# Forty instead of thirty-two tokens of an expert layer on fetched rows, and low parts of value units made in pairs

## What is computed

```python
u_g = peer_u[ic]                                   # rows picked by each token
h = gelu(einsum('chkd,cd->chk', u_g, xc)) * gc     # dot, GELU, gate
v_g = peer_v[ic]
out = einsum('chk,chkd->cd', h, v_g)               # sum of value rows
```

## Time and profile before

| | |
|---|---|
| median of 3 runs | 987.57 us |
| the profiled execution | 987.29 us, span 985.5 us |
| busy: TensorE, VectorE, ScalarE, GpSimd | 99%, 75%, 64%, 61% of the span |
| expert units | about 296 to 650 us, the gated ones from 470 |
| value units | about 650 to 978 us |
| granted clock of TensorE | 1.00 up to the last microseconds |

### The profile page before, as it was taken

The page is one execution under the profiler, slowest core; times in us unless marked ns, Lnnn a source line. Parts: engine busy times, 40 slices in busy tenths (PEclk is TensorE's granted clock), DMA queues, the critical chain, the costliest instruction groups (busy, mean ns, idle before and its releaser), DMA issues.

```text
span 985.5 us, 22607 instructions
## 1 busy us (share of the span) xinstructions
PE 975.0 (99%) x7344; PEld 918.3 (93%) x7344; DVE 743.3 (75%) x1718; ACT 626.6 (64%) x1232; POOL 598.1 (61%) x292
## 2 busy tenths in 40 slices
PE   9999999999999999999999999999999999999997
PEld 8998899999899999999999999989999999999996
DVE  7664663544747797887788888879888878888886
ACT  6774375556556666676988888865555555555553
POOL 3685624687318999989777777874443335444420
PEclk9999999999999999999999999999999999999999
DMA  7463303355545555555554444499888887988871
GB/s 264 141 238 121 128 35 107 129 188 195 204 162 171 210 203 208 211 201 209 188 189 170 170 170 170 171 355 383 311 317 316 317 309 280 333 317 313 305 276 44
DMA packets 61821, 215.05 MB, mean 218 GB/s; under 512 B 7203, under 2 KB 9251, under 8 KB 61644
## 3 DMA queue, kind: packets, MB, share of 16 engines
q1 hardware_dynamic: 51980, 180.04, 51.0%
q0 software_dynamic: 9216, 33.56, 9.4%
q10 hardware_dynamic: 576, 0.82, 0.2%
HBM read 212.89 MB, written 1.06 MB: 217 GB/s over the span
## 4 chain that ended last, share of the span: by engine, by line
PE 96%; POOL 2%; DVE 1%; ACT 1%; DMA 0%; issue 0%; ACTq 0%; DVEq 0%; POOLq 0%
PE PS L988 21%; PE PS L922 21%; PE PS L993 12%; PE PS L926 11%; PE PS L493 4%; PE PS L494 4%; PE PS L495 4%; PE PS L871 3%; PE PS L503 2%; PE PS L879 2%; PE PS L948 1%; POOL lo L1509 1%; PE PS L949 1%; PE PS L657 1%; PE PS L507 1%; PE PS L912 1%
## 5 line engine op out<-in xcount | busy, mean ns | idle before, releaser
L1509 POOL TENSOR_TENSOR lo<-raw,hi 128x1024 fp32r<-128x1024 f32 x191 | 459.4, 2413 | 152.7 <-ACT hi L1069 139.2
L922 PE MATMUL PS<-xb,hi 128*128 128x448 f32 x1024 | 235.0, 371 | 0.0
L1069 ACT CAST hi<-raw 128x1024 fp32r<-128x1024 f32 x203 | 212.7, 1048 | 33.2 <-DMA raw<-in_u_units 12.4
L988 PE MATMUL PS<-xb,hi 128*128 128x448 f32 x1008 | 228.7, 368 | 0.0
L922 PEld LDWEIGHTS PS<-xb,hi 128*128 128x128 f32 x1024 | 183.0, 189 | 12.2
L988 PEld LDWEIGHTS PS<-xb,hi 128*128 128x128 f32 x1008 | 179.9, 189 | 11.8
L2176 DVE TENSOR_TENSOR lo<-raw,hi 128x1024 fp32r<-128x1024 f32 x126 | 154.1, 1223 | 24.2 <-ACT hi L1406 24.1
L1443 ACT CAST xb<-arena 128x224 fp32r (+1 forms) x126 | 47.9, 380 | 143.6 <-PE PS L993 142.3
L926 PEld LDWEIGHTS PS<-xb,lo 128*128 128x128 f32 x1024 | 133.8, 191 | 4.7 <-POOL lo L1509 0.7
L993 PEld LDWEIGHTS PS<-xb,lo 128*128 128x128 f32 x1008 | 132.7, 191 | 4.1
L1406 ACT CAST hi<-raw 128x1024 fp32r<-128x1024 f32 x128 | 133.9, 1046 | 3.4 <-DMA raw<-in_v_units 3.4
(11 more groups left out here) (353 smaller groups left out, 1517.0 us busy)
## 6 DMA issues: line engine op xcount, KB each, us to landing
raw<-in_u_units SPq DMA_DIRECT2D x128, 512.0 KB
raw<-in_v_units SPq DMA_DIRECT2D x128, 512.0 KB
raw<-in_w_in_units SPq DMA_DIRECT2D x43, 512.0 KB
raw<-in_w_q_units SPq DMA_DIRECT2D x16, 512.0 KB
raw<-in_w_proj_units SPq DMA_DIRECT2D x8, 512.0 KB
raw<-in_w_out_units SPq DMA_DIRECT2D x8, 512.0 KB
arena<-bias_rows SPq DMA_DIRECT2D x2, 512.0 KB, 5.0
arena<-in_subkeys_t SPq DMA_DIRECT2D x1, 1024.0 KB, 5.4
```

The source lines that it names most:

```text
L922: mm(o[:, 0:2 * TD].rearrange("p (s t) -> p s t", s=2), hi[:, w, P * k:P * k + P], xb[:, k, :, 0:TD], start=(k == 0), stop=False, skip_gro ...
L988: return mm(PS[:, V_BANKS[c], 0:2 * TD].rearrange("p (s t) -> p s t", s=2), hi[:, (U_V + j) % 4, P * c:P * c + P], coef_slot(u + j)[:, :, ...
L1069: nc.scalar.copy(hi[:, j, :], raw[:, j, :]).then_inc(hi_made, 1)
L1509: nc.gpsimd.tensor_tensor(lo[:, w, :], raw[:, w, :], hi[:, w, :].bitcast(F32), ALU.subtract).then_inc(lo_pool, 1)
```

## The change

- Tokens on fetched rows: 40, in groups of 32 and 8. TD becomes 216, wide matmuls 432 columns, low ones 216. The units with gate products are 54 instead of 56 (68 to 121); FIRST stays 68, GATED_UNITS 60.
- Rows and picks of 32 tokens are repeated 4 times as before, those of 8 tokens 16 times. On SyncE's queue, at the same place, stand 3 + 15 copies of rows and 4 + 16 of picks, 38 transfers instead of 7.
- 80 fetches, dots and sums instead of 64: `ROW_WORK` does first the 8 dots of the second group, then 32 dots, then the 8 and the 32 sums. `ROWS_AFTER` spreads them: 1.31 after each pair of units, the last after pair 61.
- VectorE makes `gl` and `lo` for two units with one instruction each (`make_gl_pair`, `value_operands`), after waiting for the second unit's high parts. Slots are laid out so that a pair is one access pattern.
- ScalarE applies two GELUs to the dots instead of one, and makes four copies of rows instead of two at unit 4. The tail has two fp32 products for each chunk.

```diff
-TG = 32
+GROUPS = [32, 8]
+TG = sum(GROUPS)
 TD = T - TG
 SECOND = TD // 4
-FIRST = NKEYS - SECOND - 4
+FIRST = 68
 GATED_UNITS = NKEYS - FIRST
-REPS = P // TG
-GATHERS = P // REPS
+REPEATS = [P // tokens for tokens in GROUPS]
+GATHERS = sum(GROUPS)
+COLUMNS = [slice(0, GROUPS[0]), slice(GROUPS[0], GATHERS)]
+PICKS_IN = 16 * (2 * sum(REPEATS) - 2)
...
-        taker = con[:, C_BLK:C_BLK + TG]
-        picks = con[:, C_BLK + TG:C_BLK + TG + 2 * GATHERS].rearrange("p (a b) -> p a b", a=2)
+        takers = [con[:, C_BLK:C_BLK + GROUPS[0]], con[:, C_CEN + 2 * GATHERS:C_CEN + 2 * GATHERS + GROUPS[1]]]
+        picks = con[:, C_BLK + GROUPS[0]:C_BLK + GROUPS[0] + 2 * GATHERS].rearrange("p (a b) -> p a b", a=2)
         pick_row, pick_gate = picks[:, 0, :].bitcast(U32), picks[:, 1, :]
-        pick_dot = con[:, C_BLK + TG + 2 * GATHERS:C_IOTA]
...
-        row_sums = hot[:].rearrange("p a b c d -> p (a b c d)")[:, D:2 * D]
+        repeated = [xrep[:], area(P * TD + 4 * D, D)]
+        row_sums = [hot[:].rearrange("p a b c d -> p (a b c d)")[:, D:2 * D], repeated[1]]
...
+        def value_pair(q, parts, more):
+
+            if q == 0:
+                return parts[:, 3::-3, :]
+            return parts[:, 1:3, :] if q == 1 else more[q - 2]
...
-            sp.wait_ge(xrep_sb, 2)
-            for q in range(1, REPS):
-                sp.dma_start(xrep[TG * q:TG * q + TG, :], xrep[0:TG, :]).then_inc(picks_in, 16)
+            sp.wait_ge(xrep_sb, 4)
+            for rows, n, times in zip(repeated, GROUPS, REPEATS):
+                for q in range(1, times):
+                    sp.dma_start(rows[n * q:n * q + n], rows[0:n]).then_inc(picks_in, 16)
             sp.wait_ge(staged_made, 2)
             sp.wait_ge(picks_ps, 3)
-            for q in range(REPS):
-                sp.dma_start(picks[TG * q:TG * q + TG], staged[P - TG:P, :, GATHERS * q:GATHERS * q + GATHERS]
-                             ).then_inc(picks_in, 16)
+            for n, times, columns_of, at in zip(GROUPS, REPEATS, COLUMNS, (P - TG, P - GROUPS[1])):
+                for q in range(times):
+                    sp.dma_start(picks[n * q:n * q + n, :, columns_of], staged[at:at + n, :, n * q:n * q + n]
+                                 ).then_inc(picks_in, 16)
...
-            with pe.Fori(FIRST // 4 + 1, NKEYS // 4 - 1) as i:
+            with pe.Fori(FIRST // 4 + 1, NKEYS // 4 - 2) as i:
                 for j in range(4):
                     pe.wait_ge(coef_made, 4 * i + (j - FIRST - 3 + 2))
                     gated_unit(i, j)
+            for j in range(4):
+                pe.wait_ge(coef_made, GATED_UNITS - 8 + j - 3 + 2)
+                if GATED_UNITS - 8 + j < SECOND:
+                    gated_unit(NKEYS // 4 - 2, j)
+                else:
+                    expert_unit(NKEYS // 4 - 2, j)
...
-                    pe.wait_ge(taker_made, 1)
+                    pe.wait_ge(taker_made, 2)
                     pe.wait_ge(rows_used, 2 * GATHERS)
                 low_value(6, c)
                 low_value(7, c)
-                mm(PS[:, V_BANKS[c], 2 * TD:2 * TD + TG], row_sums[:, P * c:P * c + P], taker, start=False, stop=True,
-                   skip_group_check=True).then_inc(acc_done, 1)
+                for n, columns_of in enumerate(COLUMNS):
+                    last = mm(PS[:, V_BANKS[c], 2 * TD + columns_of.start:2 * TD + columns_of.stop],
+                              row_sums[n][:, P * c:P * c + P], takers[n], start=False, stop=True, skip_group_check=True)
+                last.then_inc(acc_done, 1)
...
-                nc.scalar.copy(xrep[0:TG, 512 * b:512 * b + 512], PS[0:TG, 2 + b, :]).then_inc(xrep_sb, 1)
+                for rows, columns_of in zip(repeated, COLUMNS):
+                    nc.scalar.copy(rows[0:columns_of.stop - columns_of.start, 512 * b:512 * b + 512],
+                                   PS[columns_of, 2 + b, :]).then_inc(xrep_sb, 1)
...
+            with act.Fori(1, 3) as i:
+                for j in range(8):
+                    value_ahead(i, j)
+            act.wait_ge(rows_used, GROUPS[1])
+            nc.scalar.activation(pick_dot[:, early_dots], pick_dot[:, early_dots], ACT.Gelu).then_inc(dots_gelu, 1)
+            with act.Fori(3, DOTS_DONE) as i:
                 for j in range(8):
                     value_ahead(i, j)
             for j in range(4):
-                value_ahead(GATHERS // 4, j)
-            act.wait_ge(rows_used, GATHERS)
-            nc.scalar.activation(pick_dot, pick_dot, ACT.Gelu).then_inc(dots_gelu, 1)
+                value_ahead(DOTS_DONE, j)
+            act.wait_ge(rows_used, LAST_DOT + 1)
+            nc.scalar.activation(pick_dot[:, late_dots], pick_dot[:, late_dots], ACT.Gelu).then_inc(dots_gelu, 1)
...
-                rows, n = (u_rows if g < GATHERS else v_t.rearrange("n p d -> (n p) d")), g % GATHERS
+                dots, n = ROW_WORK[g]
+                rows = u_rows if dots else v_t.rearrange("n p d -> (n p) d")
...
-            with dve.Fori(1, SECOND // 4 - 1) as i:
+            def dot(g):
+
+                group = 0 if g >= GROUPS[1] else 1
+                n = ROW_WORK[g][1]
+                dve.wait_ge(rows_in[g % 4], 16 * (g // 4) + 16)
+                V.scalar_tensor_tensor(out=rows_at[g % 4], in0=rows_at[g % 4], scalar=1.0, in1=repeated[group], op0=ALU.mult,
+                                       op1=ALU.mult, accum_out=pick_dot[:, n:n + 1]).then_inc(rows_used, 1)
...
-            def make_gl(i, j):
-                dve.wait_ge(gh_made, 4 * i + (j + 1))
-                low_and_high = coef_slot(4 + j)
-                V.tensor_tensor(low_and_high[:, 1, 0:TD], coef[:, 4 * i + j, :], low_and_high[:, 0, 0:TD].bitcast(F32),
-                                ALU.subtract).then_inc(gl_made, 1)
-
-            def dot(b, s):
-
-                dve.wait_ge(rows_in[s], 16 * b + 16)
-                V.scalar_tensor_tensor(out=rows_at[s], in0=rows_at[s], scalar=1.0, in1=xrep[:], op0=ALU.mult, op1=ALU.mult,
-                                       accum_out=pick_dot[:, bass.ds(4 * b + s, 1)]).then_inc(rows_used, 1)
-
-            def row_added(b, s):
-
-                dve.wait_ge(rows_in[s], 16 * b + 16)
-                dve.wait_ge(rows_used, 4 * b + s)
-                V.scalar_tensor_tensor(out=row_sums, in0=rows_at[s], scalar=pick_coef[:, bass.ds(4 * b + (s - GATHERS), 1)],
-                                       in1=row_sums, op0=ALU.mult, op1=ALU.add).then_inc(rows_used, 1)
-
-            def value_operands(i, j):
-                make_gl(2 * i + j // 4, j % 4)
-                dve.wait_ge(hi_made, 8 * i + (U_V + j + 1))
-                V.tensor_tensor(value_slot(j), value_raw(j), hi[:, (U_V + j) % 4, :].bitcast(F32), ALU.subtract).then_inc(lo_dve, 1)
+            def make_gl_pair(i, j):
+                dve.wait_ge(gh_made, 4 * i + (j + 2))
+                V.tensor_tensor(xb[:, j:j + 2, 1, 0:TD], coef[:, bass.ds(4 * i + j, 2), :], xb[:, j:j + 2, 0, 0:TD].bitcast(F32),
+                                ALU.subtract).then_inc(gl_made, 2)
...
+            def row_added(g):
+
+                n = ROW_WORK[g][1]
+                sums = row_sums[0 if n < GROUPS[0] else 1]
+                dve.wait_ge(rows_in[g % 4], 16 * (g // 4) + 16)
+                if n in (0, GROUPS[0]):
+                    V.tensor_scalar(sums, rows_at[g % 4], pick_coef[:, n:n + 1], None, ALU.mult).then_inc(rows_used, 1)
+                    return
+                dve.wait_ge(rows_used, g)
+                V.scalar_tensor_tensor(out=sums, in0=rows_at[g % 4], scalar=pick_coef[:, n:n + 1], in1=sums, op0=ALU.mult,
+                                       op1=ALU.add).then_inc(rows_used, 1)
+
+            def pick_coefs(n):
+
+                dve.wait_ge(dots_gelu, 2 - n)
+                part = COLUMNS[n]
+                link(V.tensor_tensor(pick_coef[:, part], pick_dot[:, part], pick_gate[:, part], ALU.mult))
+
+            def value_operands(i, q):
+                make_gl_pair(2 * i + q // 2, q % 2 * 2)
+                dve.wait_ge(hi_made, 8 * i + (U_V + 2 * q + 2))
+                V.tensor_tensor(value_pair(q, lo, lo_pairs), value_pair(q, raw, raw_pairs), value_pair(q % 2, hi, None).bitcast(F32),
+                                ALU.subtract).then_inc(lo_dve, 2)
...
-            value_operands(0, 2)
-            value_operands(0, 3)
-            dve.wait_ge(picks_in, 16 * (2 * REPS - 1))
-            dot(0, 0)
-            value_operands(0, 4)
-            dot(0, 1)
-            value_operands(0, 5)
-            dot(0, 2)
-            value_operands(0, 6)
-            value_operands(0, 7)
-            dot(0, 3)
-            with dve.Fori(1, GATHERS // 4) as b:
-                for j in range(8):
-                    value_operands(b, j)
-                    if j % 2:
-                        dot(b, j // 2)
-
-            first = GATHERS // 4
-            for j in range(4):
-                value_operands(first, j)
-            dve.wait_ge(dots_gelu, 1)
```

(93 more changed lines are left out.)

26 lines of the change are left out of this document (8 added, 18 removed).

## The result

The changed kernel takes 997.59 us at the median (995.92 to 998.48, 4 runs) against 987.81 us of the kernel before (4 runs, one more than in the table above): a ratio of 1.0096, 95% interval 1.0079 to 1.0114. The forecast was 994.5 us, slower by a stop at unit 79 or 80, with a range of 982 to 1002. Direction and mechanism came out; nearly every size was off, in both directions.

A forecast was written before the change was run, and what follows sets the result against it. TensorE, busy 99%, was taken to bound the kernel. Terms of -10.5 us (columns, gated units, value start, tail), +15.5 queue stall and +2.0 clock gave +7.0 on 987.57: 994.5 us, range 982 to 1002.

The forecast's parts named there:

- The stop at unit 79: 31 more copies on SyncE's queue before unit 80's load stop TensorE at unit 79 or 80 for 15.5 us; 66%.
- I take 0.5 each, between the two: Each small copy on SyncE's queue takes 0.5 us, between a store's 0.38 and the same lines' transfers at 0.71.
- Rival (a): Small issues on SyncE's queue are cheap, 0.1 to 0.2 us each: 980 to 983 us, at none 977; 17%.
- The clock: Behind the stop TensorE runs about 4 us at half speed, losing 2.0 us (0 to 2.5).
- Fewer columns: Wide matmuls 16 columns shorter in 256 units gain 13.2 us, by the slope from 448 to 512 columns.
- the low matmuls gain nothing: Low matmuls, 8 columns shorter, stand on weight loading and gain 0, with 0 to 4.6 us for the range.
- Two gated units and GpSimd's row: Expert stage's end: two fewer gated units save 1.05 us, but GpSimd's low parts and gathers allow only 0.7; net 0.35.
- Value unit 2: Start of the value stage: the paired low parts wait for unit 3's high part, so TensorE waits 1.5 us.
- The tail: A second small fp32 product in each of eight chunks costs 1.2 to 1.8 us, taken as 1.5.
- (b): The low matmuls shrink too, by 4.6 us, with the stall: 990 us; 7%.
- (c): The value stage becomes bound by transfers, needing 345 GB/s; if only 325 came through, 1007.5 us; 6%.
- (d): Pairing makes VectorE late by 0.5 us in every fourth pair, with the stall: 1002.5 us; 4%.

The follow-up runs named there:

- Experiments 1 to 3: experiment 1, experiment 2, and a third: the kernel before with its 7 copies cut into 28 of 8 partitions, 1005.88 us, ratio 1.018.
- experiment 2: The changed kernel with only the 20 copies of picks spread, the 18 of rows left in one row: 982.67 us, ratio 0.9942.
- the repeat of experiment 1: The kernel of experiment 1 once more, all value units in pairs, beside other kernels on one chip: 973.88 us, ratio 0.9844.
- experiment 1: The changed kernel with its 38 copies spread, one behind each load of units 80 to 117: 972.15 us, ratio 0.984.
- experiment 4: The kernel before with part of the value stage's columns left out, 16 units per width; two runs, only distances between starts read: 2.524 us a unit at 448, 2.447 at 432.
- Experiment 6: experiment 1 with value units 2 and 3 single, two copies behind each load, first four gathers behind units 108, 112, 116, 120: 968.97 us, ratio 0.9804.

## Why the prediction was right, and where its sizes were not

- **The stop at unit 79.** The reading of the earlier trace rows held: no slack, so each microsecond of queue is one of TensorE. Experiments 1 to 3 show it three ways, one of them without the change. The size failed in "I take 0.5 each, between the two". It was 0.68 and 0.72, the upper bound: 21.7 us of queue and a stop of 22.3 instead of 15.5. The step took a store of 8 partitions to DRAM as a neighbour; the transfers of the very lines that are multiplied were the nearer row, and partitions made little difference: at the median 0.59 us for rows and 0.67 for picks from 32 partitions in the kernel before, 0.63 for rows from 8 and 0.69 for picks, most of them from 8, in the changed one.
- **Rival (a)** falls with it: 0.57 to 0.84 us were measured for the changed kernel's copies within SBUF, 0.33 for a load. The Trainium skill's figure for dispatch in DMA: Bandwidth & Descriptors, "Anatomy of one DMA", about 50 ns, stands there for transfers that GpSimd issues. The prediction applied it to SyncE's queue, for which that section has none, and 31 of them would have made 978.7 us, not near 977.
- **The clock** fell as forecast. 3.3 us of TensorE's work ran at 1.2 GHz instead of about 4, and the loss was 1.2 us in unit 80 against its neighbours and 0.2 in the gate products ahead of it, instead of 2.0 in all. A second fall behind value unit 2 was not in the sum. It came behind idle times of 2.56 us in the changed kernel, 2.03 in experiment 2 and 1.81 in the repeat of experiment 1, and not behind 1.02 in experiment 1 itself.
- **Fewer columns.** The term of 13.2 us was mis-sized. 256 units at 0.075 to 0.077 us are 19.4. Not all of it shows in the table: from unit 0 to 79 the gain is 5.2 of 5.9 us, since unit 68, the first with gate products, took 3.68 us instead of 3.15 and unit 56 took 2.75 instead of 2.59. In three of the runs with 40 tokens unit 68 took 3.13; why it varies was not tried. The line from 512 to 448 columns doesn't go on to 432 (experiment 4). That the low matmuls gain nothing was right, by the earlier trace rows and by the widths.
- **Two gated units and GpSimd's row.** Unit 81 to value unit 0 gained 4.0 us, of which 47 units' columns are 3.6: 0.4 net, and net 0.35 was forecast. Experiment 6 shows that the row of gathers held back the rest.
- **Value unit 2.** Forecast 1.5 us; 1.3 and 2.1 in the two profiles of experiment 1, 3.4 in the changed kernel, where unit 3's transfer landed later. Unit 3 lost about 1 more by the clock. What sets the transfer's time was not tried.
- **The tail.** 1.5 us forecast. From value unit 126 on it is 1.4, with the columns of the last two units already gained.
- **Rivals (b), (c), (d).** None occurred. From 700 to 900 us the value stage carries 350 to 358 GB/s at a share of 0.96 to 0.97 and keeps its pitch of 2.45: 345 had been worked out against 366. That is close to full; whether more fetched tokens would meet that next was not tried.

Two errors of 6 us, the columns (too small a gain) and the copies (too small a loss), cancelled in part; that the total came within 3 us is luck of this kind.

## What to carry to other kernels

Count what a change adds to a queue that also carries the bottleneck's loads, issue by issue, and look for the load that stands behind it: 31 more copies, an estimated 0.2% of the bytes by their shapes, cost more than the 18 us that the change gained elsewhere. Spread over the loads behind which the queue is idle, the same copies cost nothing. For the price of an issue take the same kind of transfer at the same place, and don't scale it with its bytes or partitions. An instruction that serves two units starts when the later one is ready; at the start of a stage, where operands come one by one, keep them single; here pairing bought nothing later on either.

## What the hardware showed that was not expected

- A copy within SBUF holds SyncE's queue 0.51 to 0.71 us at the median of a kind and run (0.51 to 0.95 one by one), from 8 partitions or from 32, alone or in a row; a 512 KB load to 128 partitions holds it 0.33.
- A matmul's cost is not linear in its columns: at 448, 432 and 416 columns a unit of eight wide and eight low ones takes 2.524, 2.447 and 2.413 us.
- Matmuls with new 128 x 128 weights each have a floor: 64 of only 128 columns start 111 ns apart, and eight low and eight wide ones take 2.52 us whether the low ones have 128 columns or 224 (experiment 4).
- TensorE's clock fell to 1.2 GHz for 3.4 us behind single idle times of 1.81, 2.03 and 2.56 us at the start of the value stage, in three kernels that had run at 2.4 before, and stayed up behind one of 1.02.
